# First attention of a two-layer block: two heads at once in the array's two halves, with one score product of up to 384 local columns for each

## The reference

```python
valid = (jnp.abs(qpos - kpos) <= WINDOW) & (kpos >= 0) & (kpos < S)
s_loc = jnp.einsum('bnqgrd,bnkgd->bngrqk', qb, kb) * scale
s_loc = jnp.where(valid[None, :, None, None], s_loc, NEG_INF)
s_ctx = jnp.einsum('bnqgrd,bkgd->bngrqk', qb, k_ctx) * scale
...
p = jax.nn.softmax(jnp.concatenate([s_loc, s_ctx, s_sink], axis=-1).astype(jnp.float32), axis=-1)
o = (jnp.einsum('bngrqk,bnkgd->bnqgrd', p[..., :n_loc], vb)
     + jnp.einsum('bngrqk,bkgd->bnqgrd', p[..., n_loc:n_loc + L], v_ctx))
```

## Time and profile before

| | |
|---|---|
| median of 3 runs | 2590.11 us (2587.64 to 2590.7) |
| profiled execution | 2586.88 us, its span 2585.1 us |
| busy, share of the span | PE 96%, weight loads 78%, DVE 62%, ACT 37%, POOL 4% |
| mean granted clock of TensorE | 0.986 of 2.4 GHz |
| first attention | about 115 to 294 us of the span |

### The profile page before, as it was taken

The page is one execution under the profiler, slowest core; times in us unless marked ns, Lnnn a source line. Parts: engine busy times, 40 slices in busy tenths (PEclk is TensorE's granted clock), DMA queues, the critical chain, the costliest instruction groups (busy, mean ns, idle before and its releaser), DMA issues.

```text
span 2585.1 us, 45779 instructions
## 1 busy us (share of the span) xinstructions
PE 2470.0 (96%) x19548; PEld 2017.3 (78%) x19548; DVE 1592.5 (62%) x2468; ACT 954.8 (37%) x1630; POOL 115.0 (4%) x220
## 2 busy tenths in 40 slices
PE   6999878779999999999999999999999999999998
PEld 3777667668888888887767888888888776888887
DVE  4555577776766898864676756645455467744434
ACT  4544433323235323332554442222233255523323
POOL 0000001111100010000000000000000000000000
PEclk8999899989999999999999999999999999999999
DMA  6100000004653565420002123333332101222220
GB/s 287 66 1 1 34 4 4 4 4 171 233 193 129 191 217 197 178 78 33 1 34 82 66 74 131 131 131 130 123 98 94 49 33 73 106 99 106 94 78 33
DMA packets 32777, 244.87 MB, mean 95 GB/s; under 512 B 3680, under 2 KB 3840, under 8 KB 21568
## 3 DMA queue, kind: packets, MB, share of 16 engines
q1 hardware_dynamic: 12672, 167.97, 16.3%
q0 software_dynamic: 19904, 73.97, 9.1%
HBM read 239.83 MB, written 2.10 MB: 94 GB/s over the span
## 4 chain that ended last, share of the span: by engine, by line
PE 89%; DVE 7%; issue 2%; ACT 2%; DMA 1%; DVEq 0%; SPq 0%; ACTq 0%
PE ps L345 61%; PE ps L2436 2%; PE ps L2671 2%; PE ps L2699 1%; PE ps L1071 1%; PE ps L1493 1%; PE ps L2715 1%; PE ps L2717 1%; PE ps L2716 1%; PE ps L1027 1%; PE ps L1466 1%; PE ps L1073 1%; PE ps L1072 1%; PE ps L1051 1%; PE ps L1510 1%
## 5 line engine op out<-in xcount | busy, mean ns | idle before, releaser
L345 PE MATMUL ps<-hh,ws 128*128 128x512 f32 x3312 | 770.3, 391 | 4.1 <-DVE xT L1937 3.2
L345 PEld LDWEIGHTS ps<-hh,ws 128*128 128x128 f32 x3312 | 618.4, 188 | 136.2 <-issue 7.7
L326 ACT ACTIVATE ws<-raw 128x1024 fp32r<-128x1024 f32 x295 | 309.5, 1050 | 406.7 <-PE ps L345 386.9
L334 DVE TENSOR_TENSOR ws<-raw,ws 128x1024 fp32r<-128x1024 f32 x295 | 359.8, 1220 | 132.2 <-ACT ws L326 132.0
L345 PE MATMUL ps<-g,ws 128*128 128x512 f32 (+1 forms) x1560 | 355.8, 386 | 0.0
L345 PEld LDWEIGHTS ps<-g,ws 128*128 128x128 f32 x1560 | 287.5, 188 | 57.4
L345 PE MATMUL ps<-gg,ws 128*128 128x512 f32 x960 | 219.6, 389 | 0.0
L345 PEld LDWEIGHTS ps<-gg,ws 128*128 128x128 f32 x960 | 180.1, 188 | 37.5
L1937 DVE SCALAR_TENSOR_TENSOR xT<-ps,mods,xT 128x512 f32<-128x512 f32 x119 | 89.2, 750 | 170.6 <-PE ps L345 167.7
L2173 DVE TENSOR_TENSOR sq<-sq 128x512 f32<-128x512 f32 (+1 forms) x128 | 80.0, 625 | 127.2 <-ACT sq L2141 122.2
L2141 ACT ACTIVATE sq<-ps 128x512 f32<-128x512 f32 (+1 forms) x122 | 65.9, 540 | 238.7 <-PE ps L345 232.2
(11 more groups left out here) (418 smaller groups left out, 3532.0 us busy)
## 6 DMA issues: line engine op xcount, KB each, us to landing
raw<-in_w_m SPq DMA_DIRECT2D x32, 2048.0 KB, 7.6
raw<-in_w_ada POOLq DMA_DIRECT2D x80, 512.0 KB, 4.0
raw<-in_w_mlp SPq DMA_DIRECT2D x16, 2048.0 KB, 8.0
ar<-in_w_ada POOLq DMA_DIRECT2D x48, 512.0 KB, 3.9
raw<-in_w_in SPq DMA_DIRECT2D x8, 2048.0 KB, 7.4
raw<-in_w_mg SPq DMA_DIRECT2D x8, 1536.0 KB, 7.2
raw<-in_w_out SPq DMA_DIRECT2D x6, 2048.0 KB, 7.8
raw<-in_w SPq DMA_DIRECT2D x5, 2048.0 KB, 8.6
```

The source lines that it names most:

```text
L326: e.activation(w_of(n)[0], pieces[n][2], ACT.Copy).then_inc(*hi(n))
L334: e.tensor_tensor(l, pieces[n][2], h.bitcast(F32), ALU.subtract).then_inc(*lo(n))
L345: m = e.matmul(o, a, b, start=n == 0, stop=n == 3 * kt - 1)
```

## The change

Two heads form one step g, 16 steps instead of 32. The scores of both are issued alternately: both masks, both local products, both context products. The mask is one bf16 product over all local columns, with a stretch of zeros for the query's own block, and the local keys are one product of 256 or 384 columns which accumulates on it. Local columns now stand before the context's. The weighted sums of a pair are one visit, in the step after. Three fifths of a step's parts stand before its transposes, the rest behind them. ACT and DVE take both heads' exponentials and maxima first, and what a flow needs of them is placed anew.

```diff
-            for n in range(NI + 8):
-                yield n - 1, steps[n] if n < len(steps) else [], {what: at[what][n] for what in at}
+            for g in range(NI // 2 + 4):
+                two = (2 * g, 2 * g + 1)
+                yield g, sum((steps[n] for n in two if n < len(steps)), []), {what: at[what][two[0]] + at[what][two[1]]
+                                                                             for what in at}
...
-            for t in ps.take(("a1s", i), (PAIRS[i % 2],), 2):
-                e.wait_ge(*t)
-            o = ps.two(("a1s", i))
+            for i in pair_:
+                for t in ps.take(("a1s", i), (PAIRS[i % 2],), 2):
+                    e.wait_ge(*t)
             kbs = keys_of(qb)
-            for j, kb in enumerate(kbs):
-                oj = o[:, 256 + j * 128:384 + j * 128]
-                if kb != qb:
-                    e.matmul(oj, identb, maskb[:, 0 if kb < qb else 1, :], start=True, stop=False)
-                e.matmul(oj, q, ka[sl, kb * 128:kb * 128 + 128], start=kb == qb, stop=True)
-            e.matmul(o[:, 0:256], q, kac[sl, :], start=True, stop=True).then_inc(*acc(("a1s", i)))
+            n, at = 128 * len(kbs), 128 * (kbs[0] - qb + 1)
+            for i in pair_:
+                e.matmul(scores_of(i)[:, 0:n], identb, maskb[:, at:at + n], start=True, stop=False)
+            for i in pair_:
+                sl = halves(items[i][2])
+                e.matmul(scores_of(i)[:, 0:n], qa[sl, t4, qb * 128:qb * 128 + 128],
+                         ka[sl, kbs[0] * 128:kbs[0] * 128 + n], start=False, stop=True)
+            for i in pair_:
+                sl = halves(items[i][2])
+                e.matmul(scores_of(i)[:, n:n + 256], qa[sl, t4, qb * 128:qb * 128 + 128], kac[sl, :], start=True,
+                         stop=True).then_inc(*acc(("a1s", i)))
...
+            for g, parts, _ in attention_steps():
+                if g < NI // 2:
+                    pe_attention_scores(e, g)
+                if 1 <= g <= NI // 2:
+                    pe_attention_out(e, 2 * g - 1, 0)
+                    pe_attention_out(e, 2 * g - 1, 1)
+                early = (3 * len(parts) + 4) // 5
+                for f, k in parts[:early]:
                     pe_flow_part(e, f, k, banks)
-                if i + 1 < NI:
-                    pe_attention_scores(e, i + 1)
-                for f, k in parts[1:]:
+                if g < NI // 2:
+                    pe_attention_turn(e, 2 * g)
+                    pe_attention_turn(e, 2 * g + 1)
+                for f, k in parts[early:]:
                     pe_flow_part(e, f, k, banks)
...
+                if g < NI // 2:
+                    act_attention_exp(e, 2 * g)
+                    act_attention_exp(e, 2 * g + 1)
+                for f in late["conv"]:
+                    n, m, j, c, dst = flow(f)
+                    act_conv(e, n, m, j, c, dst)
+                for f in late["conv"]:
+                    split_hi(e, min(piece_after(f), 18))
+                if g < NI // 2:
+                    act_attention_turned(e, 2 * g)
+                    act_attention_turned(e, 2 * g + 1)
                 for f in late["tanh"]:
                     act_silu(e, f)
...
+            for g, parts, late in attention_steps():
+                if g < NI // 2:
+                    dve_attention_max(e, 2 * g)
+                    dve_attention_max(e, 2 * g + 1)
+                    dve_attention_weights(e, 2 * g)
+                    dve_attention_weights(e, 2 * g + 1)
```

More of the change, by code:

```diff
@@ L1049, in pe_attention_out @@
                 for p in range(2):
-                    vt = va[:, 4 + j, halves(p)] if j < 2 else va[:, kbs[j - 2], halves(p)]
+                    vt = va[:, kbs[j] if j < nt - 2 else 6 + j - nt, halves(p)]
                     m = e.matmul(ps["a1o", qb][halves(p), t4 * 128:t4 * 128 + 128], vt, ptb[(i - 1 + p) % 4][:, j, :],
@@ L1081, in tensor_attention @@
             e.wait_ge(*dve["mb"])
[L1082 to L1090, removed]
+            for g, parts, _ in attention_steps():
[6 more added lines that the diff above has]
+                for f, k in parts[:early]:
                     pe_flow_part(e, f, k, banks)
-                if i + 1 < NI:
-                    pe_attention_scores(e, i + 1)
-                for f, k in parts[1:]:
+                if g < NI // 2:
+                    pe_attention_turn(e, 2 * g)
+                    pe_attention_turn(e, 2 * g + 1)
+                for f, k in parts[early:]:
                     pe_flow_part(e, f, k, banks)
-                if i == NI:
+                if g == NI // 2:
                     tensor_gates(e, next(banks))
-                if i == NI + 2:
+                if g == NI // 2 + 1:
                     tensor_decays(e)
@@ L1115, in act_attention_exp @@
                 e.wait_ge(*acc["a1t", j - 2])
-            e.activation(pbuf[j % 2][:, 0:n], ps.two(("a1s", j))[:, 0:n], ACT.Exp, bias=nm,
+            e.activation(pbuf[j % 2][:, 0:n], scores_of(j), ACT.Exp, bias=nm,
                          accum_out=su).then_inc(*act(("a1s", j)))
@@ L1141, in scalar_attention @@
             split_hi(e, 11)
-            for i, parts, late in attention_steps():
-                if 0 <= i - 1 < NI:
-                    act_attention_turned(e, i - 1)
+            for g, parts, late in attention_steps():
[10 more added lines that the diff above has]
+                    act_attention_turned(e, 2 * g + 1)
                 for f in late["tanh"]:
                     act_silu(e, f)
-                for f in late["conv"]:
-                    n, m, j, g, dst = flow(f)
-                    act_conv(e, n, m, j, g, dst)
-                if i + 1 < NI:
-                    act_attention_exp(e, i + 1)
-                for f in late["conv"]:
-                    split_hi(e, min(piece_after(f), 18))
-                if i == NI + 3:
+                if g == NI // 2 + 2:
                     scalar_gates(e)
@@ L1162, in dve_attention_max @@
                 e.wait_ge(*dve["a1p", j - 4])
-            e.reduce_max(nm, ps.two(("a1s", j))[:, 0:width_of(j)], AXX).then_inc(*dve())
+            e.reduce_max(nm, scores_of(j), AXX).then_inc(*dve())
             e.wait_ge(*dve.prev())
@@ L1186, in vector_attention @@
             e.wait_ge(*dve["nsink"])
-            for i, parts, late in attention_steps():
-                if 0 <= i < NI:
-                    dve_attention_weights(e, i)
-                for f in late["silu"]:
-                    dve_silu(e, f)
-                if i + 1 < NI:
-                    dve_attention_max(e, i + 1)
-                if 3 <= i < NI + 3 and i % 2 == 0 and items[i - 3][1] == 3:
-                    qb = items[i - 3][0]
+            for g, parts, late in attention_steps():
+                if g < NI // 2:
[3 more added lines that the diff above has]
+                    dve_attention_weights(e, 2 * g + 1)
+                if 1 <= g <= NI // 2 and items[2 * g - 1][1] == 3:
+                    qb = items[2 * g - 1][0]
                     e.wait_ge(*acc["a1o", qb])
@@ L1198, in vector_attention @@
                                   ps["a1o", qb].rearrange("p (t q) -> p t q", t=4)).then_inc(*dve(("a1o", qb)))
-                for f in late["taps"]:
-                    n, m, j, g, dst = flow(f)
-                    dve_conv(e, n, m, j, g, dst)
                 for f in late["conv"]:
                     split_lo(e, min(piece_after(f), 18))
-                if i == NI + 1:
+                for f in late["taps"]:
+                    n, m, j, c, dst = flow(f)
+                    dve_conv(e, n, m, j, c, dst)
+                for f in late["silu"]:
+                    dve_silu(e, f)
+                if g == NI // 2 + 1:
                     vector_gates(e)
-                if i == NI + 3:
+                if g == NI // 2 + 2:
                     vector_decays(e)
-                if i == NI + 4:
                     vector_gated(e)
```

21 lines of the change are left out of this document (12 added, 9 removed).

## The result

| | before | changed |
|---|---|---|
| median | 2588.88 us (2585.81 to 2590.7, 4 runs) | 2548.61 us (2546.14 to 2549.9, 4 runs) |
| ratio | | 0.9855, 95% interval 0.9838 to 0.9871 |
| profiled execution, its span | 2586.88 us, 2585.1 us | 2546.14 us, 2544.4 us |
| mean granted clock | 0.986 | 0.992 |
| first score product, first token product | 114.96, 294.11 us | 116.31, 257.09 us |

The change saves 40.3 us by the medians and 40.7 by the profiled pair.

What follows compares the result with a forecast made beforehand. The prediction took TensorE to bound the kernel. Its work was to fall by 34.8 us, less 0.8 for waits, 1.7 at the start, 0.5 at the end and 1.0 for the clock: 30.8 us saved, forecast 2559.3 us, range 2553 to 2570.

## What to carry to other kernels

Count groups of products by array mode as well as products: here the regrouping, with the same instructions in fewer and longer groups, was worth about as much as the overlap of the halves: of the 36.1 us of work, 15.6 are the halves and 5.2 the wide product, which leaves 15.3 (a pair of heads fell from 3.28 to 2.77 us by grouping, the transposes by 0.25 a pair, and a visit of sums is worth 0.35). Two heads of 64 features in the two halves cost the time of one; what then has to be found is some 3.7 us of other work (183.31 to 187.54 us here, less the first head's transposes) of TensorE between scores and transposes, and it should be in place in the first step too. When a small change is forecast, take its size from a stage that repeats to 0.3 us, and give the range the spread of the rest besides.

## What the hardware showed unexpectedly

Products in different halves of the array run past one another: issued second in line, head 1's local product started 13 ns after head 0's and before head 0's context product. A bf16 product of 384 columns in front of another costs 0.17 us, and each f32 pass of 384 columns 0.32, alone in the array or with a partner in the other half. A drop in the granted clock (0.91 over 18 us) came in both profiles of the kernel before and in none of the three of the changed one, although PE's longest pause there grew from 1.1 to 2.0 us; a kernel that differs from the changed one in the order of issue alone had it again, in one profile. What brings it is not shown.
